# Moving one key unit from the pool branch to the output projection, splitting six mixed rows one tile earlier, and pooling before the last split, in a hybrid decoder step

## The chip, the cores and the metric

The kernel runs on one core of one Trainium2 chip. The metric is the device time of one execution in microseconds (us), lower being better. Engines are called PE (TensorE), DVE (VectorE), ACT (ScalarE), POOL (GpSimd) and SP (the queue that issues most DMAs); ACT has a DMA queue of its own, in order with its other work.

## What is computed

One inference step of one hybrid decoder layer, in float32, for 512 prompt tokens and 8 requests of 4 new tokens: 544 tokens of width 2048.

```python
h = rmsnorm(x, norm_mix)
proj = h @ w_in                                   # q | k | v | z_A | alpha | beta | u | z_B
...                                               # group A: gated delta rule on q, k, v -> o_a (1024 wide)
pooled, pool_new = multiscale_pool(proj[..., COL_U:COL_ZB], pool_buf, pos0, pool_w, pool_scale)
o_b = pooled * jax.nn.silu(proj[..., COL_ZB:])    # group B: trailing means over 2/4/8/16 tokens, a map per group
x = x + jnp.concatenate([o_a, o_b], axis=-1) @ w_out
h2 = rmsnorm(x, norm_cross)
qx = (h2 @ w_cq).reshape(bsz, t_len, X_HEADS, X_HEAD_DIM)
scores = jnp.einsum('bthd,bmhd->bhtm', qx, mem_k).astype(jnp.float32) * (X_HEAD_DIM ** -0.5)
probs = jax.nn.softmax(scores, axis=-1).astype(x.dtype)
ctx = jnp.einsum('bhtm,bmhd->bthd', probs, mem_v).reshape(bsz, t_len, D_MODEL)
x = x + ctx @ w_co
```

The new tokens attend to keys from a cache, `cache_mem_k`: 8 requests of 256 keys by 2048. They are stored key by key, and the score product needs them turned, width by key. Turning them is background work that the kernel spreads over earlier stages.

## The kernel before

**Tiles of three products.** Activations lie width by token, as 16 rows (row k is 128 widths by 544 tokens). A weight tile is 2048 by 128. A float32 product is made of three: each operand is split into a high part, rounded for PE, and a low part, the rest. ACT makes the high part of a weight tile (`cast_high`, L262), DVE the low part (`split_low`, L272), and PE multiplies high by high, high by low and low by high, for 16 rows and two halves of 272 tokens: 96 matmuls a tile (`multiply`, L288). Tiles are numbered through the kernel. Those of the pool branch are 64 to 79, four for each channel group g = 0 to 3 (two for z_B, q = 0 and 1, and two for u, q = 2 and 3); the output projection has 80 to 95; 96 to 99 begin the query projection, which then goes on with products of smaller parts (L2303). Results alternate between two pairs of PSUM banks, so the result of a tile must be read before PE begins the tile after next (`pj_read`).

**The order** is written out by hand: each engine has one list for each stage, and semaphores tie them. Each weight tile is loaded four tiles ahead by SP (`load_ahead`, L240). Beside the tiles of group g in the pool branch:

- In tiles q = 2 and 3 ACT copies u from PSUM to `ux` (L1762 to L1766), and only one `ux` exists: the second copy waits (`d_tile`) until DVE has made the pooled differences of the first (`dve_windows`, L1809 to L1822). POOL copies the new tokens from `ux` into `ucol` (L1873), and PE turns `ux` and `ucol` (`pe_ux`, L1879 and L1880) after row 4 of tile q = 3 for the first half of the group, and after row 11 of the next group's first tile for the second. For the last group that second turn stands after row 2 of tile 80.
- PE's map of the group (`pe_map`, L1892, 16 matmuls) comes in the next group's second tile; for the last group after row 7 of tile 80. DVE then finishes two of the rows `mixo` (L1831).
- The 16 rows `mixo` are the output projection's input. They are split in five parts: ACT's `mix_take_high` (L1794) and DVE's `mix_take_low` (L1799). Their order and their waits are a table, `MIX_PARTS`. Rows 0 to 5 of `mix_hi` lie where the key buffers `kin` and `kout` are, so that part waits for all stores of the pool branch's keys. Tile 80 starts when four parts are done, and its row 14 waits for the fifth.

```python
            pe.wait_ge(mix_low, 4)
                    steps = {2: [pe_ux(NG - 1, 1)], 7: [pe_map(NG - 1)], 13: [split(5)]}
```

**Keys.** A unit in the pool branch is 1024 widths of one request's 256 keys: 1 MB, four loads (L1646, two issued by SP and two by ACT), two turns on DVE (`dve_keys`, L1656), eight stores (L1652, half by SP and half by ACT). Step n = 4(g − 1) + q stores unit n − 1 and loads unit n, at the end of tile q's list on ACT, SP and DVE. A unit of the output projection (`load_late_units`, `dve_keys_late`) is half as large, 512 widths; step i stands at tile 80 + i, with its load in step i and its turn and stores in step i + 1. On DVE the turn stands ahead of the addition of that tile's result to the residual (`x`, L2021), on ACT the DMAs stand behind the normalised high part and the square of the result (L1997, L2000), and ahead of the cast of the weights of the tile after next. The query projection's DVE list (L2209 and on) follows directly on the last tile's.

Of the kernel before, what the change touches and what calls it, by code (L numbers as in the profile page):

```python
# [128 lines left out]
def build(nc, t):  # L129
    with ExitStack() as ctx:  # L130
# [9 lines left out]
        def area(start, end):  # L140

            pos = [start]

            def take(name, shape, dtype=F32):
                n = int(np.prod(shape))
                o = put(name, shape, dtype, pos[0])
                pos[0] += -(-n // 8) * 8
                assert pos[0] <= end, (name, pos[0], end)
                return o
            take.pos = pos  # L150
            return take
# [43 lines left out]
        def at_least(eng, s, v):  # L195

            if not (isinstance(v, int) and v <= 0):
                if isinstance(s, Reused):
                    eng.wait_ge(s.sem, s.at(v))
                else:  # L200
                    eng.wait_ge(s, v)
# [62 lines left out]
        def split_low(dve, stage, j, q):  # L264

            n = FIRST[stage] + j + q // 4
            q = q % 4
            if isinstance(n, int) and 4 * n >= NTILE:
                return
            dve.wait_ge(hi_cast, 4 * n + q + 1)  # L270
            lo, w = (low_wide, raw_wide) if is_mem(n) else (low, raw)
            dve.tensor_tensor(lo[q][:], w[q][:], high_of(n, q)[:].bitcast(F32), ALU.subtract).then_inc(lo_split, 1)  # L272
# [504 lines left out]
        def sample3(x):  # L777

            return x[:, SEQ:TOK].rearrange("p (b t) -> p b t", b=NB)
# [847 lines left out]
            "d_tile", "pw_loaded", "pooled", "ob_done", "mix_high", "mix_low", "old_rows"))  # L1627

        BLOCKS = MEM // T32
        POOL_UNITS = 10  # L1630
        OUT_UNITS = 12
        take = area(M_DELTA + 2 * 2 * P, M_HIMIX + 6 * TOK)
        kin = take("kin", [BLOCKS, 2 * P])
        kout = [take(f"kout{i}", [4, BLOCKS, T32]) for i in range(2)]
# [1 line left out]
        k_turned = Reused(conv_step, 9 * HEADS)  # L1636
        k_late_loaded = Reused(const_loaded, 16 + 64 * POOL_UNITS)
        k_late_stored = [Reused(xts_stored, 80 + 64 * POOL_UNITS), Reused(kts_stored, 64 + 64 * POOL_UNITS)]
        k_late_turned = Reused(conv_step, 9 * HEADS + 2 * POOL_UNITS)

# [7 lines left out]
        def keys_out(eng, src, b, tile, step, first, n, stored, quarters):  # L1648

            for i in quarters:  # L1650
                dst = keysT_d[b, first * T32:(first + n) * T32, tile + step * i, :].rearrange("(j d) m -> d j m", d=T32)
                eng.dma_start(dst, src[i * T32:(i + 1) * T32].rearrange("p j g m -> p j (g m)")).then_inc(stored.sem, 16)  # L1652
# [7 lines left out]
        def load_units(sp, n, quarters):  # L1660

            if 0 < n <= POOL_UNITS:
                sp.wait_ge(k_turned.sem, k_turned.at(2 * n))
                for f in range(2):
                    keys_out(sp, kout[f], (n - 1) // 2, 8 * ((n - 1) % 2) + f, 2, 0, 4, k_stored[f], quarters)
            if n < POOL_UNITS:
                if n == 0:
# [3 lines left out]
        def dve_keys(dve, n):  # L1671

            if 0 < n <= POOL_UNITS:
                dve.wait_ge(k_in_loaded.sem, k_in_loaded.at(64 * n))
                for f in range(2):
                    at_least(dve, k_stored[f], 64 * (n - 1))
                    keys_turn(dve, kout[f], kin[:, :, f * P:(f + 1) * P]).then_inc(k_turned.sem, 1)

        def u_sample(x):
            return x[:, BUF + SEQ:UN].rearrange("p (b s) -> p b s", b=NB)  # L1680
# [44 lines left out]
        def act_pool(act):  # L1725
            def body(g):
                first = is_first(g)
                for q in range(4):
# [15 lines left out]
                    if g == 1 and q == 2:  # L1744
                        mix_take_high(act, 0)
                    if g == 2 and q == 2:
                        mix_take_high(act, 1)
                    if g == 3 and q == 2:
                        mix_take_high(act, 2)
# [26 lines left out]
            act.activation(ust[0:BUF, 0, :], pj[0:BUF, 2 * i, 0:P], ACT.Copy)  # L1776
            act.activation(ust[0:NS, 1, :], pj[0:NS, 2 * i, P:2 * P], ACT.Copy).then_inc(ust_ready, 1)

        MIX_PARTS = ((6, 8), (8, 12), (12, 14), (0, 6), (14, 16))

        def mix_take_high(act, m):

            a, b = MIX_PARTS[m]
            if m in (0, 3):
                act.wait_ge(oa_done, HEADS)
            else:
                act.wait_ge(ob_done, (0, 4, 6, 0, 8)[m])
            if m == 3:
                for s in k_stored:
                    act.wait_ge(s.sem, s.at(64 * POOL_UNITS))  # L1790
                act.wait_ge(k_turned.sem, k_turned.at(2 * POOL_UNITS))
            if m == 4:
                act.wait_ge(ust_stored, 16 * 9 * 8)
            act.activation(mix_hi[:, a:b, :], mixo[:, a:b, :], ACT.Copy).then_inc(mix_high, 1)  # L1794

        def mix_take_low(dve, m):
            a, b = MIX_PARTS[m]
            dve.wait_ge(mix_high, m + 1)
            dve.tensor_tensor(mix_lo[:, a:b, :], mixo[:, a:b, :], mix_hi[:, a:b, :].bitcast(F32), ALU.subtract).then_inc(mix_low, 1)  # L1799

        def dve_windows(dve, g, i):

            n = 2 * g + i
            dve.wait_ge(pj_read, 4 * (16 + g) + 2 + i + 1)
            src = ux[:]
            for m in range(g + 1):
                dst = (us_a, us_b)[m % 2][:]
                lo = (2 << m) - 1
                dve.tensor_tensor(dst[:, lo:UN], src[:, lo:UN], src[:, lo - (1 << m):UN - (1 << m)], ALU.add).then_inc(win_step, 1)  # L1809
                wn[0] += 1  # L1810
                dve.wait_ge(win_step, wn[0])
                src = dst
            other = (us_b, us_a)[g % 2][:]
            if i == 0:
                at_least(dve, pooled, g)
            iw = 1.0 / WINDOWS[g]
            dve.tensor_tensor(other[:, 0:16], src[:, BUF:BUF + 16], cst[:, C_INV + 16 * g:C_INV + 16 * g + 16], ALU.mult).then_inc(win_step, 1)
            wn[0] += 1
            dve.wait_ge(win_step, wn[0])
            dve.tensor_tensor(dpool[:, i, 0:16], other[:, 0:16], ux[:, BUF:BUF + 16], ALU.subtract)  # L1820
            dve.scalar_tensor_tensor(dpool[:, i, 16:SEQ], src[:, BUF + 16:BUF + SEQ], iw, ux[:, BUF + 16:BUF + SEQ], ALU.mult, ALU.subtract)
            dve.scalar_tensor_tensor(sample3(dpool[:, i]), u_sample(src)[:, :, BUF:USEG], iw, u_sample(ux[:])[:, :, BUF:USEG],  # L1822
                                     ALU.mult, ALU.subtract).then_inc(d_tile, 1)
        wn = [0]

        def dve_map(dve, g):

            dve.wait_ge(pooled, g + 1)
            for d in range(2):
                o = halves(mixo[:, 8 + 2 * g + d, :])  # L1830
                dve.scalar_tensor_tensor(o, dk[:, 2 * d:2 * d + 2, 0:HALF], gain[:, G_POOL + 2 * g + d:G_POOL + 2 * g + d + 1],  # L1831
                                         o, ALU.mult, ALU.mult).then_inc(ob_done, 1)

        def dve_pool(dve):
            for g in range(NG):
                for q in range(4):
                    if g > 0:
                        split_low(dve, "pool", g, q + 1)
                    else:
                        dve_delta(dve, HEADS - 1, q, lambda: split_low(dve, "pool", 0, q + 1), lambda: None)  # L1840
                    if g > 0 and q == 0:
                        dve_windows(dve, g - 1, 1)
                    if g > 0 and q == 1:
                        dve_map(dve, g - 1)
                    if g > 0 and q == 2:
                        mix_take_low(dve, g - 1)
                    if q == 3:
                        if g == 3:
                            mix_take_low(dve, 3)
                        dve_windows(dve, g, 0)  # L1850
                    if g > 0:
                        dve_keys(dve, 4 * (g - 1) + q)

# [84 lines left out]
        def load_late_units(sp, i, quarters):  # L1938

            if 1 < i <= OUT_UNITS + 1:  # L1940
                sp.wait_ge(k_late_turned.sem, k_late_turned.at(2 * (i - 1)))
                b, h = divmod(2 * POOL_UNITS + i - 2, XH)
                for f in range(2):
                    keys_out(sp, kout_late[f], b, 4 * h, 1, 2 * f, 2, k_late_stored[f], quarters)
            if 0 < i <= OUT_UNITS:
                if i == 1:
# [4 lines left out]
        def dve_keys_late(dve, i):  # L1951

            if 1 < i <= OUT_UNITS + 1:
                dve.wait_ge(k_late_loaded.sem, k_late_loaded.at(64 * (i - 1)))
# [209 lines left out]
        def t_cast(act, S, idx):  # L2164
            kh, m = divmod(T_ORDER[idx], KH)
            act.wait_ge(S.t_step.sem, S.t_step.at(4 * idx + 4))
            if S is CQ and idx == 0:
                for s in k_late_stored:
                    act.wait_ge(s.sem, s.at(64 * OUT_UNITS))
            act.activation(q_t[kh][:, :, 0, m, :], q_tt[idx % 2][:], ACT.Copy).then_inc(S.t_high.sem, 1)  # L2170
# [136 lines left out]
        def sp_cq(sp):  # L2307
# [13 lines left out]
            for s in k_late_stored:  # L2321
                sp.wait_ge(s.sem, s.at(64 * OUT_UNITS))
            sp.wait_ge(part_done.sem, part_done.at(77))
# [864 lines left out]
```

## Time and profile before

| | |
|---|---|
| median of 3 runs | 1657.14 us (1656.83 to 1658.19) |
| the profiled execution | 1655.45 us |
| its span (first to last instruction) | 1653.6 us |
| granted TensorE clock, mean | 0.994 of full speed |
| PE busy | 1619.4 us, 98% of the span |
| pool branch, tiles 64 to 79 | about 765 to 971 us |
| output projection, tiles 80 to 95 | 975.7 to 1177.6 us |

The profile gives the busy time of each engine, who waited for whom, and each instruction with its start and length. A weight-tile matmul with 272 tokens starts 0.125 us after the one before it at full clock, though each is listed as longer, since they overlap. An idle PE is the one thing that counts directly; idle time elsewhere costs only if PE waits behind it.

### The profile page before, as it was taken

What the parts mean: (1) busy time and instruction counts of PE and PEld (TensorE: products, weight loads), DVE (VectorE), ACT (ScalarE), POOL (GpSimd) and SP (SyncE); (2) the same over time, 40 slices, a digit from 0 to 9 for tenths busy, and PEclk for the clock granted to TensorE, in tenths of its full rate; (3) what the DMA queues carried; (4) which work ended last, traced back from release to release, by engine and by line L of the source; (5) the groups of instructions that cost most, each with busy time, mean ns of one, the idle gap of its engine ahead of it and who ended that gap; (6) DMA issues with size and microseconds to landing.
All of it is one profiled execution on the core that took longest, in us unless ns stands there. A gap on an engine that the chain in (4) does not pass through costs nothing.

```text
span 1653.6 us, 31288 instructions
## 1 busy us (share of the span) xinstructions
PE 1619.4 (98%) x12650; PEld 1499.8 (91%) x12650; DVE 987.4 (60%) x1689; ACT 657.5 (40%) x1115; POOL 180.6 (11%) x191
## 2 busy tenths in 40 slices
PE   7999999999999999999999989999999999899998
PEld 5887899999999999999999989999999995499998
DVE  5676446765756647566344553444688853399952
ACT  5566345353452544425422222222343322235542
POOL 0121001111121111211100001111000000001120
PEclk9999999999999999999999999999999999999999
DMA  7898634233242432324389965787323359953462
GB/s 267 258 303 254 212 92 113 70 94 101 68 117 52 117 92 77 92 55 126 83 205 240 231 167 156 205 237 212 116 77 102 97 225 419 360 153 104 130 184 108
DMA packets 320670, 263.35 MB, mean 159 GB/s; under 512 B 15049, under 2 KB 287314, under 8 KB 315234
## 3 DMA queue, kind: packets, MB, share of 16 engines
q1 hardware_dynamic: 298752, 245.21, 49.9%
q10 hardware_dynamic: 21826, 16.87, 3.7%
q8 instruction: 63, 1.03, 0.3%
q14 instruction: 29, 0.24, 0.0%
HBM read 218.09 MB, written 44.30 MB: 159 GB/s over the span
## 4 chain that ended last, share of the span: by engine, by line
PE 84%; DVE 5%; DMA 4%; SPq 3%; ACT 1%; issue 1%; ACTq 1%; POOL 0%; DVEq 0%
PE pj L288 43%; PE pj L487 10%; PE pj L2303 7%; PE dk L2303 5%; DMA kin<-in_cache_mem_k_dram 2%; PE pj L3057 2%; PE dk L2567 2%; PE pj L2600 1%; DMA values_raw_b<-in_cache_mem_v_dram 1%; DVE kout L1656 1%; PE dk L1273 1%; PE pj L2578 1%; PE dk L1279 1%; SPq L1701 1%; PE dk L826 1%
## 5 line engine op out<-in xcount | busy, mean ns | idle before, releaser
L288 PE MATMUL pj<-a_hi,w_high 128*128 128x272 f32 x1792 | 394.1, 301 | 1.4 <-DVE w_low L272 1.4
L288 PE MATMUL pj<-a_hi,w_low 128*128 128x272 f32 x1792 | 370.2, 288 | 0.0
L288 PE MATMUL pj<-a_lo,w_high 128*128 128x272 f32 x1792 | 369.7, 288 | 0.0
L272 DVE TENSOR_TENSOR w_low<-w_raw,w_high 128x2048 fp32r<-128x2048 f32 x76 | 173.9, 2288 | 203.5 <-ACT w_high L262 203.4
L288 PEld LDWEIGHTS pj<-a_hi,w_high 128*128 128x128 f32 x1792 | 280.9, 189 | 15.0 <-issue 8.1
L288 PEld LDWEIGHTS pj<-a_lo,w_high 128*128 128x128 f32 x1792 | 281.6, 188 | 0.0
L288 PEld LDWEIGHTS pj<-a_hi,w_low 128*128 128x128 f32 x1792 | 280.2, 189 | 0.1
L262 ACT ACTIVATE w_high<-w_raw 128x2048 fp32r<-128x2048 f32 x76 | 145.5, 1915 | 140.9 <-issue 82.6
L288 PE MATMUL pj<-mix_hi,w_high 128*128 128x272 f32 x512 | 107.1, 291 | 4.0 <-issue 4.0
L2187 ACT ACTIVATE q_high<-q_part 128x512 fp32r<-128x512 f32 x140 | 77.5, 621 | 74.0 <-DVE q_part L2241 36.6
L288 PE MATMUL pj<-mix_lo,w_high 128*128 128x272 f32 x512 | 106.8, 290 | 0.0
L288 PE MATMUL pj<-mix_hi,w_low 128*128 128x272 f32 x512 | 106.2, 289 | 0.0
L272 DVE TENSOR_TENSOR w_low_wide<-w_raw_wide,w_high_wide 128x2048 fp32r<-128x2048 f32 x32 | 73.1, 2287 | 40.4 <-ACT w_high_wide L262 40.4
L2248 DVE TENSOR_TENSOR q_low<-q_part,q_high 128x512 fp32r<-128x512 f32 x140 | 93.0, 709 | 4.0 <-ACT q_high L2187 3.3
L288 PEld LDWEIGHTS pj<-mix_hi,w_high 128*128 128x128 f32 x512 | 81.5, 191 | 4.3 <-issue 4.2
L262 ACT ACTIVATE w_high_wide<-w_raw_wide 128x2048 fp32r<-128x2048 f32 x32 | 61.2, 1914 | 52.6 <-PE pj L487 44.0
L288 PEld LDWEIGHTS pj<-mix_hi,w_low 128*128 128x128 f32 x512 | 81.3, 190 | 0.0
L288 PEld LDWEIGHTS pj<-mix_lo,w_high 128*128 128x128 f32 x512 | 81.3, 191 | 0.0
L487 PE MATMUL pj<-w_high_wide,hm_lo 128*128 128x512 f32 x248 | 78.9, 399 | 0.0
L487 PE MATMUL pj<-w_high_wide,hm_hi 128*128 128x512 f32 x248 | 77.0, 391 | 0.0
L2241 DVE TENSOR_TENSOR q_part<-q_part 128x512 f32<-128x512 f32 x80 | 58.7, 734 | 22.1 <-DMA q_part<-in_w_cq_dram 17.8
L487 PE MATMUL pj<-w_low_wide,hm_hi 128*128 128x512 f32 x248 | 64.2, 394 | 0.0
(468 smaller groups left out, 2916.0 us busy)
## 6 DMA issues: line engine op xcount, KB each, us to landing
w_raw<-in_w_in_dram SPq DMA_DIRECT2D x48, 1024.0 KB, 6.0
w_raw_wide<-in_w_ck_dram SPq DMA_DIRECT2D x16, 1024.0 KB, 9.0
w_raw_wide<-in_w_cv_dram SPq DMA_DIRECT2D x16, 1024.0 KB, 7.1
w_raw<-in_w_out_dram SPq DMA_DIRECT2D x16, 1024.0 KB, 8.4
q_part<-in_w_cq_dram SPq DMA_DIRECT2D x48, 256.0 KB, 3.7
w_raw<-in_w_co_dram SPq DMA_DIRECT2D x8, 1024.0 KB, 6.2
q_part<-in_w_co_dram SPq DMA_DIRECT2D x32, 256.0 KB, 3.7
kin<-in_cache_mem_k_dram ACTq DMA_DIRECT2D x20, 256.0 KB, 6.2
```

The costliest lines, as they stand in the source:

```text
L262: act.activation(high_of(n, q)[:], w[q][:], ACT.Copy).then_inc(hi_cast, 1)
L272: dve.tensor_tensor(lo[q][:], w[q][:], high_of(n, q)[:].bitcast(F32), ALU.subtract).then_inc(lo_split, 1)
L288: mm = pe.matmul(pj[:, 2 * (q % 2) + b, 0:n], wt[:, k, :], x(k, o, n), start=(k == 0 and m == 0), stop=(k == KT - 1 and m == 2))
L487: mm = pe.matmul(pj[:, 2 * (j % 2) + m, :], x[:, KW * q + k, m * P:(m + 1) * P], wt[:, k, :], start=(q == 0 and u == 0), stop=(q == 3 and ...
L826: mm = pe.matmul(dk[0:64, b, 0:HALF], wt[:, k, :], x[:, k, b * HALF:(b + 1) * HALF], start=(k == 0 and m == 0), stop=(k == KT - 1 and m == 2))
L1273: mm = pe.matmul(dk[:, i, 0:HALF], ones, SQ[:, i // 2, (i % 2) * HALF:(i % 2 + 1) * HALF], start=True, stop=True)
L2187: act.activation(part_high[:, q_slot(n)], q_parts[G % 2][:, o], ACT.Copy).then_inc(S.part_cast.sem, 1)
L2241: dve.tensor_tensor(w[:, o], w[:, a], w[:, b], op).then_inc(S.part_step.sem, 1)
L2248: dve.tensor_tensor(part_low[G % 2][:, o], q_parts[G % 2][:, o], part_high[:, q_slot(n)].bitcast(F32), ALU.subtract).then_inc(S.part_split ...
L2303: mm = pe.matmul(q_bank(o), w[:, m, :], v, start=(kh == 0 and m == 0 and u == 0), stop=(kh == 1 and m == KH - 1 and u == 2))
L2567: mm = pe.matmul(scp(h)[:, i // 2, (i % 2) * 256:(i % 2) * 256 + 256], qx[:, DT * h + d, i * P:(i + 1) * P], ktb[h % 2][:, d, :], start=(d ...
L3057: mm = pe.matmul(half_product(u), wt[:, k, :], x[:, k, part], start=(k == 0 and m == 0), stop=(k == KT - 1 and m == 2))
```

## The change

Three edits, all in the lists around tiles 76 to 95.

1. `POOL_UNITS` goes from 10 to 9 and `OUT_UNITS` from 12 to 14: the last 1 MB unit of the pool branch becomes two of the output projection's half-size units. The keys turned are the same.
2. `MIX_PARTS` changes order: rows 0 to 5 are split third, in the third tile of the last group (tile 78), and rows 12 and 13 fourth, in tile 79. The waits in `mix_take_high` follow: the wait for the key stores now stands in tile 78's list.
3. In tile 79's list on DVE the pooling sums (`dve_windows(dve, 3, 0)`) come ahead of the fourth split.

```diff
-        POOL_UNITS = 10
-        OUT_UNITS = 12
+        POOL_UNITS = 9
+        OUT_UNITS = 14
...
-        MIX_PARTS = ((6, 8), (8, 12), (12, 14), (0, 6), (14, 16))
+        MIX_PARTS = ((6, 8), (8, 12), (0, 6), (12, 14), (14, 16))
...
-            if m in (0, 3):
+            if m in (0, 2):
                 act.wait_ge(oa_done, HEADS)
             else:
-                act.wait_ge(ob_done, (0, 4, 6, 0, 8)[m])
-            if m == 3:
+                act.wait_ge(ob_done, (0, 4, 0, 6, 8)[m])
+            if m == 2:
                 for s in k_stored:
                     act.wait_ge(s.sem, s.at(64 * POOL_UNITS))
...
                     if q == 3:
+                        dve_windows(dve, g, 0)
                         if g == 3:
                             mix_take_low(dve, 3)
-                        dve_windows(dve, g, 0)
```

**Where the instructions move.** PE's and POOL's lists are the same as before. First, ACT's list beside tiles 78 and 79, before and then with the change (`w_high_58<-w_raw_52` is tile 79's cast, `w_high_57<-w_raw_49` tile 80's; `128x3264` are six mixed rows, `128x1088` two):

```order
L262 ACTIVATE w_high_58<-w_raw_52 128x2048
L1794 ACTIVATE mix_hi<-mixo 128x1088
L1762 ACTIVATE ux<-pj 128x272
L1763 ACTIVATE ux<-pj 128x240
L1764 ACTIVATE ux<-pj 128x8x4
L1766 ACTIVATE ux<-pj 128x8x15
L1652 DMA keysT_scratch<-kout_161 32x4x256 x2
L1652 DMA keysT_scratch<-kout_162 32x4x256 x2
L262 ACTIVATE w_high_57<-w_raw_49 128x2048
L1776 ACTIVATE ust<-pj 15x128
L1777 ACTIVATE ust<-pj 32x128
L1794 ACTIVATE mix_hi<-mixo 128x3264
```

```order
L262 ACTIVATE w_high_58<-w_raw_52 128x2048
L1794 ACTIVATE mix_hi<-mixo 128x3264
L1762 ACTIVATE ux<-pj 128x272
L1763 ACTIVATE ux<-pj 128x240
L1764 ACTIVATE ux<-pj 128x8x4
L1766 ACTIVATE ux<-pj 128x8x15
L262 ACTIVATE w_high_57<-w_raw_49 128x2048
L1776 ACTIVATE ust<-pj 15x128
L1777 ACTIVATE ust<-pj 32x128
L1794 ACTIVATE mix_hi<-mixo 128x1088
```

The six rows stand now ahead of the first copy of u (tile 78), the two rows where the six were, and the DMAs of the removed unit are gone.

Second, the same place on DVE, as a difference (`w_low_53` is tile 80's low part), and where the two rows' split has gone:

```order
 L1656 STREAM_TRANSPOSE kout_162<-kin 128x8x4x32
 L272 TENSOR_TENSOR w_low_56<-w_raw_52,w_high_58 128x2048
-L1799 TENSOR_TENSOR mix_lo<-mixo,mix_hi 128x1088
-L1656 STREAM_TRANSPOSE kout_161<-kin 128x8x4x32
-L1656 STREAM_TRANSPOSE kout_162<-kin 128x8x4x32
-L272 TENSOR_TENSOR w_low_53<-w_raw_49,w_high_57 128x2048
 L1799 TENSOR_TENSOR mix_lo<-mixo,mix_hi 128x3264
+L272 TENSOR_TENSOR w_low_53<-w_raw_49,w_high_57 128x2048
 L1809 TENSOR_TENSOR us_a<-ux 128x678
 L1809 TENSOR_TENSOR us_b<-us_a 128x676
```

```order
 L1821 SCALAR_TENSOR_TENSOR dpool<-us_b,ux 128x496
 L1822 SCALAR_TENSOR_TENSOR dpool<-us_b,ux 128x32
+L1799 TENSOR_TENSOR mix_lo<-mixo,mix_hi 128x1088
 L1809 TENSOR_TENSOR us_a<-ux 128x678
 L1809 TENSOR_TENSOR us_b<-us_a 128x676
```

The six rows' split comes ahead of tile 80's weights, two turns are gone, and the two rows' split stands between the two pooling sums of the last group.

Third, DVE's last two tiles of the output projection (`w_low_56` and `w_low_53` are the weights of tiles 95 and 96; `x` and `a_lo` the results):

```order
 L2023 SCALAR_TENSOR_TENSOR a_lo<-x_1_166,gain,a_hi 128x544
 L272 TENSOR_TENSOR w_low_56<-w_raw_52,w_high_58 128x2048
+L1656 STREAM_TRANSPOSE kout_late_170<-kin_late 128x8x2x32
+L1656 STREAM_TRANSPOSE kout_late_171<-kin_late 128x8x2x32
 L2021 TENSOR_TENSOR x_0_165<-pj,xr_163 128x544
 L2023 SCALAR_TENSOR_TENSOR a_lo<-x_0_165,gain,a_hi 128x544
 L272 TENSOR_TENSOR w_low_53<-w_raw_49,w_high_57 128x2048
+L1656 STREAM_TRANSPOSE kout_late_170<-kin_late 128x8x2x32
+L1656 STREAM_TRANSPOSE kout_late_171<-kin_late 128x8x2x32
 L2021 TENSOR_TENSOR x_1_166<-pj,xr_164 128x544
 L2023 SCALAR_TENSOR_TENSOR a_lo<-x_1_166,gain,a_hi 128x544
```

Turns now stand ahead of the additions of tiles 94 and 95 as well; on SP and on ACT their loads and stores are added in tiles 93 to 95.

## Rows read from the trace of the kernel before

**Rows 1.** The page: busy time, share of the span and instructions of each engine.

```profile
PE 1619.4 (98%) x12650; PEld 1499.8 (91%) x12650; DVE 987.4 (60%) x1689; ACT 657.5 (40%) x1115; POOL 180.6 (11%) x191
```

**Rows 2.** Who PE waited for from 965 to 993 us: total, times, longest.

```profile
PE pj L288 <- issue: 4.0, 1, 4.0
PE pj L1879 <- POOL ucol L1873: 2.8, 1, 2.8
```

**Rows 3.** Timeline, PE: start us, us, line, operation [idle before <-releaser].

```profile
963.01 0.27 PE L1879 MATMUL pj<-cst,ux 128*15 128x128 f32 x1
...
970.99 0.41 PE L288 MATMUL pj<-a_lo,w_high 128*128 128x272 f32 x2
971.24 0.41 PE L288 MATMUL pj<-a_hi,w_low 128*128 128x272 f32 x2
975.67 0.49 PE L288 MATMUL pj<-mix_hi,w_high 128*128 128x272 f32 x2 [4.02 <-issue]
...
982.24 0.28 PE L1879 MATMUL pj<-cst,ux 128*15 128x128 f32 x1 [2.78 <-POOL ucol L1873]
...
987.76 3.83 PE L1892 MATMUL dk<-dpool,pw 128*128 128x272 f32 x16
```

**Rows 4.** Timeline, DVE, tiles 78 to 80.

```profile
960.72 2.37 DVE L1656 STREAM_TRANSPOSE kout<-kin 128x1024 f32<-128x1024 f32 x2 [0.58 <-DMA kin<-in_cache_mem_k_dram]
...
972.01 3.56 DVE L1799 TENSOR_TENSOR mix_lo<-mixo,mix_hi 128x3264 fp32r<-128x3264 f32 x1 [2.51 <-ACT mix_hi L1794]
975.49 0.86 DVE L1809 TENSOR_TENSOR us_a<-ux 128x678 f32<-128x678 f32 x1
...
979.95 0.18 DVE L1822 SCALAR_TENSOR_TENSOR dpool<-us_b,ux 128x32 f32<-128x32 f32 x1
981.25 0.87 DVE L1809 TENSOR_TENSOR us_a<-ux 128x678 f32<-128x678 f32 x1 [1.12 <-ACT ux L1766]
```

**Rows 5.** Timeline, ACT and its DMA queue (ACTq), tiles 77 to 80.

```profile
950.42 2.13 ACTq L1652 DMA_DIRECT2D keysT_scratch<-kout  x4
...
954.69 1.91 ACT L262 ACTIVATE w_high<-w_raw 128x2048 fp32r<-128x2048 f32 x1 [6.87 <-issue]
...
959.34 0.40 ACT L1762 ACTIVATE ux<-pj 128x272 f32<-128x272 f32 x1 [1.73 <-PE pj L288]
...
969.05 2.93 ACT L1794 ACTIVATE mix_hi<-mixo 128x3264 fp32r<-128x3264 f32 x1 [1.56 <-DMA keysT_scratch<-kout]
980.31 0.40 ACT L1762 ACTIVATE ux<-pj 128x272 f32<-128x272 f32 x1 [8.32 <-DVE dpool L1822]
```

**Rows 6.** Windows of PE: stretch, length, busy (instructions), granted clock, DMA share, GB/s.

```profile
976.30:979.50 3.20, 3.16 (x15) 0.52 0.14 35
...
987.00:1195.00 208.00, 208.00 (x1654) 1.00 0.66 185
```

**Rows 7.** The chain of waits, at the last key store: start us, us, what.

```profile
964.51 4.38 DMA keysT_scratch<-kout
```

**Rows 8.** The page, costliest groups: the low part of a weight tile.

```profile
L272 DVE TENSOR_TENSOR w_low<-w_raw,w_high 128x2048 fp32r<-128x2048 f32 x76 | 173.9, 2288 | 203.5 <-ACT w_high L262 203.4
```

**Rows 9.** Timeline, DVE, last tiles of the output projection, and the query projection.

```profile
1153.31 1.30 DVE L1656 STREAM_TRANSPOSE kout_late<-kin_late 128x512 f32<-128x512 f32 x2 [2.70 <-DMA kin_late<-in_cache_mem_k_dram]
...
1177.63 0.72 DVE L2021 TENSOR_TENSOR x<-pj,xr 128x544 f32<-128x544 f32 x1 [5.81 <-PE pj L288]
...
1223.20 2.50 DVE L2248 TENSOR_TENSOR q_low<-q_part,q_high 128x512 fp32r<-128x512 f32 x4
```

**Rows 10.** The chain of waits, where the query projection's small products begin.

```profile
1226.82 6.07 PE pj L2303 x48
```

**Rows 11.** Key stores of the pool branch: time from issue to landing.

```profile
DMA to landing us min/median/max: 2.0/3.1/6.0
```

**Rows 12.** Timeline, POOL, the last two copies of the new tokens.

```profile
960.32 0.21 POOL L1873 COPY ucol<-ux 128x32 f32<-128x32 f32 x1 [38.55 <-ACT ux L1766]
981.28 0.91 POOL L1873 COPY ucol<-ux 128x32 f32<-128x32 f32 x1 [20.75 <-ACT ux L1766]
```

**Rows 13.** Key loads of the output projection, the same.

```profile
DMA to landing us min/median/max: 2.3/4.0/8.1
```

## The prediction, made before the changed kernel ran

> **What bounds the kernel now.** I read the page first: PE is busy 1619.4 us, 98% of the span [rows 1], so only what shortens PE's list or removes its waits can count, and the change leaves PE's list as it is. The next view was who PE waited for. Around the change it waits twice [rows 2]: 4.0 us, put down to nothing, and 2.8 us for POOL's `ucol`. The timeline of PE shows where [rows 3]. Pairs of matmuls start 0.25 us apart at full clock, tile 79's last at 971.24, so tile 80 could start at 971.49; it starts at 975.67, 4.18 us late. What released it is on DVE: the low part of the six rows ends at 972.01 + 3.56 = 975.57 [rows 4], the fourth of the four parts that tile 80 waits for. Then 18 matmuls on (rows 0 to 2), PE's turn of `ux` waits 2.78 us, until 982.24, because the second copy of u starts only at 980.31 [rows 5], as soon as DVE has the pooled differences of the first, whose sums stood behind the six rows (975.49 to 980.13) [rows 4].
>
> These two waits cost more than their 7 us. After the first the granted clock is 0.52 of full speed, the 1.2 GHz level, with a half-idle PE behind it [rows 6]: 18 matmuls take 982.24 − 2.78 − 975.67 = 3.79 us, where at full clock they take 18 × 0.125 = 2.25. After the second, 30 matmuls up to the map (about 982.4 to 987.76) take 5.4 us instead of 3.75 [rows 3].
>
> Then I followed back why the six rows are late. ACT's high part of them starts at 969.05 [rows 5], 0.16 us after the last store of the last pool unit lands (964.51 + 4.38 = 968.89) [rows 7]. That unit is turned on DVE until 960.72 + 2.37 = 963.09 [rows 4]. So the chain is: turn, stores, high part, low part, then the sums, the copy, the turn of `ux`, the map.
>
> **The change, part by part.** Times are on the old profile's clock.
>
> *One pool unit fewer.* The last store is now unit 8's. Its turn ended at 950.4 already, for its stores are issued from 950.42 [rows 5]. From the end of the turn to the last landing it took 968.89 − 963.09 = 5.80 us for unit 9; the same from 950.4 gives 956.2. Unit 9's loads, which would have stood right behind these stores, and its turn of 2.37 us on DVE [rows 4] are gone.
>
> *Six rows in tile 78.* ACT casts tile 79's weights until at most 954.69 + 1.91 = 956.6, some 2 us earlier without the loads to issue ahead of it [rows 5], then waits for the landing and makes the high part from 956.35 to 959.3 (2.93 us). Queued behind it is the first copy of u, which starts at 959.34 today because tile 78 ends then [rows 5]: not later, but with no room. DVE makes the low part from 959.3 to 962.9 (3.56), where today two rows and the turn stand.
>
> *Tile 80's weights and the sums.* The low part of the weights takes 2.29 us [rows 8]: 962.9 to 965.2. The sums take 4.64 us (975.49 to 980.13) [rows 4]: to 969.8. Then the low part of two rows, a third of 3.56 or about 1.2 to 1.3 us: to 971.1. PE arrives at 971.49. The wait of 4.18 us is gone, with 0.4 us to spare. This is also what the third edit does: with the two rows first, the sums would end at 971.1, which still serves the copy.
>
> *Second copy of u.* It needs tile 79 finished (971.5) and the differences (969.8). From the copy's start to PE's turn it took 982.24 − 980.31 = 1.93 us, so the turn can go at 973.4; PE arrives at 971.49 + 2.25 = 973.74. The 2.78 us go, with 0.3 to spare. The second sums start 0.94 us after the copy (981.25 against 980.31) [rows 4, 5] and end 4.64 later, at 977.1; PE reaches the map at 973.74 + 0.22 for the two turns + 3.75 = 977.7, in time. Without waits I expect no fall of the clock.
>
> The sum: 4.18 + 2.78 + (3.79 − 2.25) + (5.4 − 3.75) = 10.1 us. Against it, the map starts at 987.76 now [rows 3] and at 977.7 then: 10.1. Behind the map the order is as it was, each on the other: no further gain.
>
> *Two late units more.* Turns of 1.30 us [rows 9] now stand ahead of the additions of tiles 94 and 95, and ACT and SP have stores and loads beside them. The same work stands beside each of the tiles 82 to 93 today, and PE was busy 208.0 of 208.0 us there [rows 6]; that is the cover. What is new is its end: DVE goes straight from tile 95 (addition at 1177.63) into the query projection and has no idle until the first low part there, done at 1223.20 + 2.50/4 = 1223.8 [rows 9]. PE needs it at 1226.82 [rows 10]. A delay of 1.3 us leaves 1.7. I cost it at nothing; if loads land so late that the slack is used up, each further us costs one.
>
> What stays unmeasured is the landing of unit 8's stores in its new role. Stores of this branch land 2.0 to 6.0 us after issue [rows 11]; I take the case of unit 9 (4.38 from issue), the nearest, with the same 1 MB weight load behind it. At 2.0 nothing more is won, as PE has no wait left: gain 10.1. At 6.0 everything in tile 78 is 1.6 us later.
>
> **The copy for the new tokens, and a rule that speaks against the change.** POOL's copy takes 0.21 us at 960.32, and 0.91 at 981.28, where it started 0.03 us after a DVE addition with two inputs in SBUF (981.25, 0.87 long) and ended 0.07 after it [rows 4, 12]. So I let a copy wait for such a DVE instruction. The six rows' subtraction is one, 3.56 us long, and it starts at 959.3, before the copy at 960.3. Then the copy ends not at 960.5 but at 962.9, and PE turns it at 963.01 [rows 3]: 0.1 us to spare instead of 2.5.
> The Trainium skill, "SBUF — State Buffer", section "Who interferes with whom", says that a DVE instruction with two SBUF inputs contends with a GpSimd instruction that reads SBUF, and that the later one fully blocks. By that rule the next rival is live; without it the sum would be 10.1 us in nearly all cases. The trace agrees (0.91 against 0.21).
>
> **The rivals.**
>
> A. *The forecast*: all waits at tile 80 go. 10.1 us. For it: four margins, each positive; against it: they are only 0.1 to 0.6 us.
>
> B. *A wait in tile 79 takes their place.* The store lands late, up to 957.8; high part until 960.9, low part until 964.5, the copy for the new tokens behind it, and PE, due at 963.01, waits up to 1.5 us in tile 79. The rest of the chain moves by as much and so does PE, so tile 80 still starts without a wait. If the clock falls too, 1.5 us more, as after the old waits. Gain 7.1 to 9.5; about 1649 us. For it: DMAs are dense there, and the margin is 0.1.
>
> C. *No change that can be told.* The 4.0 us wait has no releaser named [rows 2]; if something besides the six rows holds tile 80, or if a later stage that waits for loads gives the time back, under 3.3 us remain. Against it: 975.57 and 975.67 fit closely, and later loads are issued on signals of PE's progress, so they move with it. Time 1654 to 1657 us.
>
> D. *Slower, through the last late units.* DVE, in tile 95's list, sits on a key load that is late, with the addition, the next weights and the whole preparation of the query projection behind it. It decides from 1.7 us of lateness on; to be slower than before by 0.2% it must eat the 10.1 us as well: 1.7 + 10.1 + 3.3 = 15 us. Loads there land within 8.1 us of issue [rows 13] and are issued a tile (12 us) ahead: at worst they are about a microsecond late. Time 1660 us or more.
>
> **How the numbers follow.** The profiled execution took 1655.45 us, 1.7 under the median of 1657.14; its span is 1653.6. A: span 1643.5, so a profiled time of 1645.4 and a median of 1647.0. Chances: A 0.66, B 0.22, C 0.08, D 0.04. Within 0.2% (3.3 us) is about what a measurement of this kernel can tell from no change. A and B are faster by more (0.88), C is the same, D slower. The range takes A with the spread of the runs, down to 1645.6, and B to its bad end, 1657.14 − 7.1 = 1650.0, with a little spread: 1650.5. C and D stay outside.
>
> **What would show it.** In the new profile: no wait of PE at tile 80's start and at its turn of `ux`; full clock from 960 to 985; the six rows' high part starting near 956.3 and ending at about 959.3; the copy for the new tokens in tile 79 lasting some 2.5 us rather than 0.21 (that is B's door); the first key turn of the added units ahead of the additions of tiles 94 and 95, and no PE wait around the first small products of the query projection, some 10 us earlier than today. I am wrong if tile 80 still waits, if PE waits over 2 us in tile 79, or if the 10 us are there at tile 81 and no longer at the end.

## The result and the profile after

The changed kernel takes 1647.23 us, median of 5 runs (1644.57 to 1648.36), against 1656.83 us for the kernel before, run beside it, median of 5 (1654.52 to 1658.19). The ratio is 0.9942 with a 95% interval of 0.9931 to 0.9953: about 9.6 us faster. The span of the profiled execution is 1645.4 us, against 1653.6.

The first view is again who PE waited for, now from 900 to 1000 us in the changed kernel:

```profile
PE pj L288 <- DVE w_low L272: 0.8, 1, 0.8
```

Both waits of [rows 2] are gone. The one that is left stands before tile 77, where the kernel before waits as well; the change does not touch it. The timeline of PE, where [rows 3] were read (start, length, line, operation):

```profile
963.56 0.28 PE L1879 MATMUL pj<-cst,ux 128*15 128x128 f32 x1
...
971.80 0.42 PE L288 MATMUL pj<-a_hi,w_low 128*128 128x272 f32 x2
972.05 0.41 PE L288 MATMUL pj<-mix_hi,w_high 128*128 128x272 f32 x2
...
974.30 0.27 PE L1879 MATMUL pj<-cst,ux 128*15 128x128 f32 x1
...
978.27 2.00 PE L1892 MATMUL dk<-dpool,pw 128*128 128x272 f32 x8
```

Tile 80's first matmul (`mix_hi`) starts 0.25 us after tile 79's last pair, where it was 4.43 us. The turn of `ux` in tile 80 follows without a wait, and the map starts at 978.27, not 987.76. The windows of PE (stretch, length, busy, granted clock, DMA share, GB/s) show the clock of the stretch that [rows 6] had at 0.52:

```profile
976.30:979.50 3.20, 3.20 (x23) 1.00 0.39 98
960.00:985.00 25.00, 25.00 (x188) 1.00 0.37 101
987.00:1195.00 208.00, 207.22 (x1656) 1.00 0.68 194
```

Full clock and no idle from 960 to 985; but in the output projection PE was busy 207.22 of 208 us, where it had been 208.00. This wait is the larger part of what the gain lost again, and the experiments look at it.

ACT's timeline in the same place, for [rows 5]:

```profile
950.85 2.09 ACTq L1652 DMA_DIRECT2D keysT_scratch<-kout  x4
...
956.91 2.93 ACT L1794 ACTIVATE mix_hi<-mixo 128x3264 fp32r<-128x3264 f32 x1 [1.96 <-DMA keysT_scratch<-kout]
959.75 0.38 ACT L1762 ACTIVATE ux<-pj 128x272 f32<-128x272 f32 x1
...
964.32 1.10 ACT L1794 ACTIVATE mix_hi<-mixo 128x1088 fp32r<-128x1088 f32 x1
972.25 0.40 ACT L1762 ACTIVATE ux<-pj 128x272 f32<-128x272 f32 x1 [6.84 <-PE pj L288]
```

The six rows' high part starts at 956.91, released by the last key store, and the first copy of u stands right behind it. DVE and POOL, for [rows 4] and [rows 12]:

```profile
948.44 2.37 DVE L1656 STREAM_TRANSPOSE kout<-kin 128x1024 f32<-128x1024 f32 x2 [1.29 <-DMA kin<-in_cache_mem_k_dram]
...
959.87 3.56 DVE L1799 TENSOR_TENSOR mix_lo<-mixo,mix_hi 128x3264 fp32r<-128x3264 f32 x1 [2.60 <-ACT mix_hi L1794]
963.35 2.30 DVE L272 TENSOR_TENSOR w_low<-w_raw,w_high 128x2048 fp32r<-128x2048 f32 x1
965.57 0.85 DVE L1809 TENSOR_TENSOR us_a<-ux 128x678 f32<-128x678 f32 x1
...
970.12 1.28 DVE L1799 TENSOR_TENSOR mix_lo<-mixo,mix_hi 128x1088 fp32r<-128x1088 f32 x1
973.20 0.86 DVE L1809 TENSOR_TENSOR us_a<-ux 128x678 f32<-128x678 f32 x1 [1.80 <-ACT ux L1766]
```
```profile
960.70 2.80 POOL L1873 COPY ucol<-ux 128x32 f32<-128x32 f32 x1 [38.50 <-ACT ux L1766]
973.23 0.91 POOL L1873 COPY ucol<-ux 128x32 f32<-128x32 f32 x1 [9.73 <-ACT ux L1766]
```

The six rows' low part runs from 959.87 to 963.43, and POOL's copy for the new tokens, 0.21 us long before, now takes 2.80: it ends at 963.50, 0.07 us after the subtraction. PE turns it at 963.56. The turn comes 4.04 us after tile 79's start (959.52) where it came 3.87 us after (963.01 less 959.14): the margin of 0.1 us is used up, and no more than 0.17 us paid.

Four times tell where the time went. All are from profiles: the start of PE's small transpose ahead of tile 79, the addition of tile 80's result on DVE, the first small product of the query projection on PE, and the span.

| | tile 79 starts | addition of tile 80 | first small product | span |
|---|---|---|---|---|
| before | 959.14 | 997.63 | 1226.66 | 1653.6 |
| after | 959.52 | 988.14 | 1218.48 | 1645.4 |
| gained so far | −0.38 | 9.49 | 8.18 | 8.2 |

From tile 79 to the addition of tile 80 it took 38.49 us and takes 28.62: 9.87 less. From there to the first small product it took 229.03 and takes 230.34: 1.31 more. (Each is one execution. In the two later profiles of the changed kernel the first stretch takes 28.44 and 28.43 us, since the copy held nobody up there, and the second 229.02 and 229.03.)

### The profile page after: what moved, and what is told of

It is laid out like the page before. It is cut to its first block, busy times and chain, and to the rows that moved or that the text cites. A ratio compares the mean times of both kernels' runs of the same rounds, so it can differ in the third digit from the quotient of the medians.

```text
span 1645.4 us, 31303 instructions
## 1 busy us (share of the span) xinstructions
PE 1617.3 (98%) x12650; PEld 1497.8 (91%) x12650; DVE 988.1 (60%) x1691; ACT 657.5 (40%) x1115; POOL 183.4 (11%) x191
## 4 chain that ended last, share of the span: by engine, by line
PE 81%; DMA 7%; DVE 5%; SPq 2%; ACT 2%; issue 2%; ACTq 1%; POOL 0%; DVEq 0%
PE pj L288 39%; PE pj L487 10%; PE pj L2303 7%; PE dk L2303 5%; PE pj L3057 2%; DMA kin<-in_cache_mem_k_dram 2%; DMA xr<-xT_scratch 2%; PE dk L2567 2%; DMA kin_late<-in_cache_mem_k_dram 1%; PE pj L2600 1%; DMA values_raw_b<-in_cache_mem_v_dram 1%; PE dk L1273 1%; PE pj L2578 1%; ACTq L1652 1%; PE dk L1279 1%
```

## The experiments

### The first edit alone

Against the kernel before:

```diff
-        POOL_UNITS = 10
-        OUT_UNITS = 12
+        POOL_UNITS = 9
+        OUT_UNITS = 14
```

> Only the first edit: 9 pool units and 14 late units, the old order of the mixed parts and the sums last. My theory: with unit 9 gone the six rows in tile 79's list no longer wait for a store; ACT can start their high part right after the turned rows of tile 79 (about 964), the low part ends near 970.4, so tile 80 starts on time (the 4.2 us go), but the sums behind it end near 975, the second copy of u starts there, and PE waits some 3 us at its turn after row 2 of tile 80, with a fall of the clock of up to 1.5 us behind it. Gain over the kernel before 4 to 6 us: ratio about 0.997. Rival (the units are not what held the six rows, the order is): tile 80 still starts about 4 us late, ratio 1.000. Rival (the units alone bring everything): ratio 0.994.

Measured: median 1650.73 us, ratio 0.9968 (0.9956 to 0.9979), a gain of 6.5 us. The ten times are spread widely (1647.61 to 1655.38), and the profile is of the lowest of them, so the parts below are read from the stretch itself. The waits of PE from 820 to 1260 us, and DVE's timeline, show which of the two waits the unit had caused:

```profile
PE pj L1879 <- POOL ucol L1873: 3.0, 1, 3.0
PE pj L288 <- DVE w_low L272: 1.3, 1, 1.3
```
```profile
966.86 3.56 DVE L1799 TENSOR_TENSOR mix_lo<-mixo,mix_hi 128x3264 fp32r<-128x3264 f32 x1 [2.33 <-ACT mix_hi L1794]
970.33 0.86 DVE L1809 TENSOR_TENSOR us_a<-ux 128x678 f32<-128x678 f32 x1
...
974.79 0.19 DVE L1822 SCALAR_TENSOR_TENSOR dpool<-us_b,ux 128x32 f32<-128x32 f32 x1
```

The six rows' low part ends at 970.42 instead of 975.57, tile 80 starts on time, and the second wait stays, 3.0 us, since the sums behind that part end at 974.98. From tile 79's start to tile 80's addition it takes 990.94 − 959.29 = 31.65 us: 6.84 of the 9.87 us come from the first edit, the other 3.03 need the new order; the medians say the same (6.5 of 9.6). Both rivals fall. One detail was off: I had allowed up to 1.5 us for a fall of the clock behind the wait, and there was none:

```profile
974.00:977.00 3.00, 0.06 (x1) 1.00 1.03 286
977.10:984.00 6.90, 6.90 (x45) 1.00 0.19 47
```

### The third edit undone

Against the changed kernel:

```diff
                     if q == 3:
-                        dve_windows(dve, g, 0)
                         if g == 3:
                             mix_take_low(dve, 3)
+                        dve_windows(dve, g, 0)
```

> The changed kernel with its third edit undone: in tile 79 the two mixed rows' low part stands ahead of the pooling sums again. My theory: the sums then end about 1.3 us later, near 971.5, and the second copy of u waits for the end of tile 79 (971.9) anyway; tile 80 has its four parts sooner. No difference from the changed kernel: ratio to before 0.994. Rival (the third edit carries a part of the gain): PE waits 0.5 us or more at its turn in tile 80, and the ratio is 0.995 or above.

Measured: median 1648.59 us, ratio 0.9955 (0.9935 to 0.9975), which does not tell it from the changed kernel, though the ratio alone falls on the rival's side (0.995 or above). The profile speaks for the place itself: from tile 79 to tile 80's addition 987.52 − 959.08 = 28.44 us (28.62 in the changed kernel's first profile, 28.44 and 28.43 in its other two), and PE has no wait at its turn, which was the rival's other sign. The sums ended 970.50 + 0.18 = 970.7, while the copy that needs them started at 971.64, with the end of tile 79. So the third edit carries nothing here; it moves 1.3 us of DVE work within idle time. This profile lost its time later (232.19 us from tile 80's addition to the first small product, under lists that the third edit does not touch), in the output projection; its waits of PE from 820 to 1260 us:

```profile
PE pj L288 <- DVE w_low L272: 1.5, 4, 0.6
PE pj L2303 <- DVE q_low L2248: 1.1, 1, 1.1
```

The second row is PE at the first small product of the query projection, where my fourth rival stood.

### The turn of tile 79 two rows earlier, and its control

The same edit, once against the changed kernel and once against the kernel before:

```diff
-                steps[3].setdefault(4, []).append(pe_ux(g, 0))
+                steps[3].setdefault(4 if first else 2, []).append(pe_ux(g, 0))
```

> The changed kernel with PE's turn of ux in the tiles q = 3 of groups 1 to 3 moved from after row 4 to after row 2, 1.5 us earlier. My theory (POOL's copy is held until the six rows' subtraction on DVE has ended): in tile 79 the copy ends near 963.5, PE arrives at about 962.0 and waits 1.5 us; perhaps a fall of the clock behind it. Slower than the changed kernel by 1.5 to 3 us: ratio to before 0.995 to 0.996. In groups 1 and 2 there is no such subtraction beside it and no wait. Rival (the copy is only listed as long, its result is there 0.2 us after its start): no wait of PE, ratio 0.994.

> The control: the same earlier turn in the kernel before, where no DVE subtraction runs beside the copy in tile 79. The copy ends at about 960.5 and PE comes at 961.5: no wait in tile 79, the copy 0.21 us long, time as before (within 1 us).

Measured on the changed kernel: median 1647.2 us, ratio 0.9949 (0.9929 to 0.9969). POOL's copy, the subtraction on DVE and PE's turn in tile 79:

```profile
960.60 2.81 POOL L1873 COPY ucol<-ux 128x32 f32<-128x32 f32 x1 [38.72 <-ACT ux L1766]
```
```profile
959.78 3.56 DVE L1799 TENSOR_TENSOR mix_lo<-mixo,mix_hi 128x3264 fp32r<-128x3264 f32 x1 [2.29 <-ACT mix_hi L1794]
```
```profile
963.46 0.28 PE L1879 MATMUL pj<-cst,ux 128*15 128x128 f32 x1 [1.68 <-POOL ucol L1873]
```

and in the control, on the kernel before:

```profile
960.60 0.21 POOL L1873 COPY ucol<-ux 128x32 f32<-128x32 f32 x1 [38.56 <-ACT ux L1766]
```
```profile
961.85 0.27 PE L1879 MATMUL pj<-cst,ux 128*15 128x128 f32 x1
```

Both copies start at 960.60. With the subtraction beside it the copy takes 2.81 us and ends at 963.41, 0.07 after it, and PE waits 1.68 us for it; without, 0.21 us and no wait. The copy's result is really late, not only listed so. All nine profiles in which the subtraction began first show the same: the copy takes from 1.42 to 2.81 us, depending on when it starts, and ends 0.06 to 0.08 us after the subtraction. The stretch up to tile 80's addition is 989.56 − 959.26 = 30.30 us, 1.86 more than the 28.44 of the changed kernel's undisturbed profiles. PE's turn stands 1.83 us behind its place (961.38 + 0.25 to 963.46), so the wait is all of it, and the granted clock from 963.4 to 967.0 us is 1.00. The medians do not separate 1.7 us here, for the times vary by as much; the control's single run took 1658.75 us, 1.6 above the median of the kernel before beside it where I had expected 1 at most, with 231.54 us from tile 80's addition to the first small product (998.13 to 1229.67), though it has only the twelve late units.

### Do the added units cost anything?

> The changed kernel once more, as the measure for the three beside it. Its part up to tile 80 takes what it took (addition of tile 80 near 988). What I look at is the stretch from that addition to the first small product of the query projection: 230.5 us in the changed kernel's profile, 229.2 in the one before; I expect 229 to 232, changing from run to run with where loads land.

Without the two units, against the changed kernel:

```diff
-        OUT_UNITS = 14
+        OUT_UNITS = 12
...
-            sp.dma_start(kept_keys[slot][:, first:end, :], keysT_d[b, :, first:end, :]).then_inc(kv_loaded[slot].sem, 16)
+            sp.dma_start(kept_keys[slot][:, first:end, :], keysT_d[0 if b == NB - 1 else b, :, first:end, :]).then_inc(kv_loaded[slot].sem, 16)
```

> The changed kernel without its two added late units: 9 pool units and 12 late ones; the last 1024 widths of the last request's keys are not turned, and that request is scored with keys of the first in their place. My theory: the two added units cost about 1 us, by DVE entering the query projection later and by tiles 94 and 95; this kernel is 0.5 to 1.5 us faster than the changed one beside it, and has no wait at the first small product. Rival (the added units are free, the loss of 1.3 us is the loads of the other twelve): same as the changed kernel within 0.4 us, with PE waits for low parts still there in tiles 83 to 93.

Measured: the changed kernel again 1647.11 us, ratio 0.9936 (0.9922 to 0.9949); without the two units 1647.45 us, ratio 0.994 (0.9927 to 0.9954). My expectation of 0.5 to 1.5 us fell. Without the units, the stretch from tile 80's addition to the first small product is 1220.08 − 991.05 = 229.03 us; with them, in this second profile of the same kernel, 1217.30 − 988.28 = 229.02. So the added units need not cost anything. The first profile lost 1.31 us all the same: 0.90 ahead of tile 95 (first row), 0.19 ahead of tile 94, and 0.2 that I cannot place. DVE's rows, and below them one of ACT's DMA queue, show what led to it:

```profile
1157.15 0.52 PE L288 MATMUL pj<-mix_hi,w_high 128*128 128x272 f32 x2 [0.75 <-DVE w_low L272]
```
```profile
1135.24 0.72 DVE L2021 TENSOR_TENSOR x<-pj,xr 128x544 f32<-128x544 f32 x1 [1.43 <-issue]
...
1147.93 1.30 DVE L1656 STREAM_TRANSPOSE kout_late<-kin_late 128x512 f32<-128x512 f32 x2 [3.85 <-DMA kin_late<-in_cache_mem_k_dram]
1149.15 0.69 DVE L2021 TENSOR_TENSOR x<-pj,xr 128x544 f32<-128x544 f32 x1
...
1154.80 2.29 DVE L272 TENSOR_TENSOR w_low<-w_raw,w_high 128x2048 fp32r<-128x2048 f32 x1 [3.36 <-ACT w_high L262]
```
```profile
1151.69 1.06 ACTq L1646 DMA_DIRECT2D kin_late<-in_cache_mem_k_dram  x2
```

In the kernel before, the same low part, of tile 95's weights, waits a microsecond less for ACT's high part:

```profile
1159.09 2.29 DVE L272 TENSOR_TENSOR w_low<-w_raw,w_high 128x2048 fp32r<-128x2048 f32 x1 [2.27 <-ACT w_high L262]
```

In the changed kernel's profile, tile 92's addition had waited 1.43 us for something without a name (the residual's load, as the next experiment shows) and started 3.1 us after its tile's end, so ACT's high part, its stores and its key load came late. The key load landed for a turn at 1147.93, 3.8 us after tile 93's end (1144.14, as tiles end 12.00 us apart from 988.14 on); the addition behind the turn was 5.0 us late, and the low part of tile 95's weights ended at 1157.09, 0.9 us after PE could have begun. Up to here this is work that the old unit counts have too: the turn at 1147.93 is of the twelfth late unit. But beside tile 93 ACT now also issues the thirteenth unit's loads (1.06 us) ahead of the cast of tile 95's weights; without an added unit DVE waits 2.27 us for that cast in the kernel before and 2.53 us in the version with twelve, with it 3.36 us. Some 0.8 to 1.1 us earlier, the low part would have cost PE next to nothing. So the 0.9 us at tile 95 took both: a chain late by old work, and an added unit's loads on top. In each of these profiles the lateness is handed from tile to tile, through additions, DMAs and turns, and what PE sees of it differs.

### Residual loads earlier, turns behind the additions

First on SP alone, against the changed kernel:

```diff
-                    sp_residual(sp, "out", j, q)
+                    i = 4 * j + q
+                    if i == 0:
+                        sp_residual(sp, "out", 0, 0)
+                        sp_residual(sp, "out", 0, 1)
                     if q or not is_first(j):
                         sp.wait_ge(pj_read, 80 + 4 * j + q)
                         sp_x2(sp, j if q else j - 1, (q - 1) % 4)
+                        if i < 15:
+                            sp_residual(sp, "out", (i + 1) // 4, (i + 1) % 4)
```

Then the same, and on DVE besides:

```diff
-                    dve_keys_late(dve, i)
                     dve.wait_ge(tile_done, 80 + i + 1)
...
                     dve.tensor_tensor(halves(x2[q % 2][:]), product(q), halves(xr[q % 2][:]), ALU.add).then_inc(pj_read, 1)
+                    dve_keys_late(dve, i)
```

> The changed kernel with SP's load of the residual row for tile 80+i issued one tile earlier (right behind the store of the result two before it), so that it is no longer behind the 1 MB weight load. My theory: the addition then never waits for this load (9.8 us in six waits in the changed kernel), only for key turns; PE's waits for low parts in the output projection go in part. Gain 0 to 1.3 us on the changed kernel. Rival (the key loads alone set the pace): no difference, and additions as late as before.

> The same, and on DVE the key turns behind the addition of the tile instead of ahead of it, in the gap in which DVE waits for ACT's high part. My theory: additions start with the end of their tile in all 16 tiles, ACT's list follows, no PE wait for a low part between tile 81 and the first small product; stretch 229 us or less. Gain on the changed kernel 0.5 to 2 us. Rival (the stores and loads of the keys now come later, so that turns and the low parts behind them are late instead): no gain, PE waits for low parts as before.

Measured: 1646.41 us, ratio 0.9934 (0.9921 to 0.9948), and 1645.7 us, ratio 0.9928 (0.9914 to 0.9941). DVE's waits from 985 to 1185 us in the first of the two:

```profile
DVE kout_late L1656 <- DMA kin_late<-in_cache_mem_k_dram: 30.9, 14, 3.0
DVE x L2026 <- PE pj L288: 14.6, 9, 5.8
```

No addition (now L2026) waits without a name any more, where the changed kernel had six such waits of 9.8 us in all: what they had waited for was the residual's load. With both edits, the waits and the first and the last three additions (now L2025):

```profile
DVE x L2025 <- PE pj L288: 50.4, 16, 5.8
```
```profile
987.73 0.72 DVE L2025 TENSOR_TENSOR x<-pj,xr 128x544 f32<-128x544 f32 x1 [2.05 <-PE pj L288]
...
1143.72 0.73 DVE L2025 TENSOR_TENSOR x<-pj,xr 128x544 f32<-128x544 f32 x1 [2.84 <-PE pj L288]
...
1155.72 0.73 DVE L2025 TENSOR_TENSOR x<-pj,xr 128x544 f32<-128x544 f32 x1 [2.84 <-PE pj L288]
...
1167.72 0.73 DVE L2025 TENSOR_TENSOR x<-pj,xr 128x544 f32<-128x544 f32 x1 [2.83 <-PE pj L288]
```

All 16 additions start with the end of their tile, 12.00 us apart, and none waits for a key load. In both profiles the stretch is 229.03 us (987.96 to 1216.99, 987.73 to 1216.76), without a wait of PE in it. To see whether that is time won, the last pair ran again beside the changed kernel:

> The changed kernel a third time, beside the next one, to tell apart 1.4 us. Ratio to before 0.9935 to 0.9945; the stretch from tile 80's addition to the first small product is 229 to 232 us.

> The version with the residual loads one tile earlier and the key turns behind the additions, a second time. My theory: all 16 additions 12.00 us apart again and the stretch 229.0 us, so this kernel's times are lower by about 1 us in the middle and spread less than the changed kernel's beside it; ratio to before 0.992 to 0.994. Rival (the first comparison was luck): the two medians lie within 0.5 us, or the additions are uneven again.

Measured: the changed kernel 1645.78 us, ratio 0.9934 (0.9922 to 0.9946); the version with even additions 1645.74 us, ratio 0.9935 (0.9922 to 0.9948). The rival holds: the medians are 0.04 us apart, and the stretch was 229.03 us in both profiles (989.13 to 1218.16 and 988.21 to 1217.24). The even order does in each of its profiles what it should, but often there is nothing to remove. In six profiles with 14 units and the old order in this stage, the changed kernel's three among them, the stretch was 229.0 (three times), 230.1, 230.3 and 232.2 us; in three with twelve, 229.0, 229.0 and 231.5. Above 229.03 that is 0.9 us in the mean with 14 and 0.8 with twelve, so a price of the added units is not shown; nor is it ruled out, for two of the six waited at the first small product (1.1 and 0.3 us) and none of the three did. No version was shown to beat the changed kernel.

Not tried: the second edit without the first. With ten pool units ACT's wait for the last unit's stores would stand ahead of that unit's turn on DVE, which itself stands behind the split that ACT must feed; the lists would wait on each other.

## Why the prediction was right

The median was forecast at 1647.0 and is 1647.23; forecast A is what happened. That the median is met within 0.3 us is luck. The span was worked out as 1643.5 and is 1645.4, and the 1.9 us between have three parts: 0.38 because tile 79 started that much later in this profile, 0.23 because the gain around tile 80 was 9.87 and not 10.1, and 1.31 lost in the output projection. The first is scatter ahead of the change: tile 79 starts anywhere from 959.08 to 962.61 in the twelve profiles. The median comes out right because I added 1.7 us to the profiled time, as the first profile of the kernel before lay that much below its median; here the profiled execution is the median. The gain, from kernels run side by side, is 9.6 us of the 10.1 forecast.

- *What holds tile 80.* The wait had no name in [rows 2]; I took the six rows' low part for it, from 975.57 against 975.67. Shown: with the low part ending at 970.42 in the first experiment, the wait is gone.
- *The landing of unit 8's stores.* Taken as 5.80 us after the turn's end, as for unit 9. The turn ended at 948.44 + 2.37 = 950.81 and the high part started at 956.91, so 6.1 less the 0.16 between landing and start: about 5.9. This and 0.4 us of general lateness brought everything in tile 78 half a microsecond (0.56) behind my times. PE was only 0.38 behind, and the difference is what its turn in tile 79 waited.
- *POOL's copy held by the subtraction.* Right, with its size: forecast to end 0.07 after it, and it ends 0.06 to 0.08 after it in nine profiles, with a control. The rule of the Trainium skill's page "SBUF — State Buffer", section "Who interferes with whom", that a DVE instruction with two SBUF inputs contends with a GpSimd one that reads SBUF, holds in this kernel: 2.81 us against 0.21. Rival B was as near as its margin said: the turn came 0.17 us later than undisturbed, and with PE 1.5 us earlier it waited 1.68 us.
- *The second copy and the map.* Forecast 973.74 and 977.7, measured 974.30 and 978.27: both 0.56 late, as tile 79's turn was by 0.55. These margins held; only that of the first copy did not quite.
- *The clock.* Of the 10.1 us, 3.2 were for matmuls at the lower clock. The measured 9.87 contain them; idle alone was 6.8. I had also allowed 1.5 us of clock for the shorter wait of rival B, and as much for the wait left in the first experiment; this was wrong: waits of 1.68 and 3.03 us left it at full speed.
- *The third edit.* I said that either order serves the copy. Shown: 28.44 us without it, 28.43 to 28.62 with it.
- *The late units.* Costed at nothing, with the cover that the same work stands beside tiles 82 to 93 unharmed. This is the weakest term of the sum. In the best profiles it holds (229.02 and 229.03 with and without), and the mean over the profiles shows no price. But PE's 208.00 of 208.0 us in [rows 6] was one execution, and I took it for a property of the kernel: the control with the old unit counts lost 2.5 us there. I looked for the end of the added work only in DVE's list at the first small product, where I counted 1.7 us left; with the first small product at 1226.66, not at the 1226.82 of [rows 10], it was 1.5. That was used up in two of six profiles with 14 units (waits of 1.1 and 0.3 us), so rival D's mechanism exists; it needed 15 us and shows one. What I named and gave no price is ACT's list: the added loads ahead of the cast for tile 95 were a condition of the 0.9 us in the changed kernel's first profile. And a late load took up to 9.2 us from issue there, not the 8.1 that I took as the worst.

## What to carry to other kernels

When a hand-ordered list keeps an engine waiting, look for the piece of background work whose completion the wait really needs; moving one unit of it to a stage with room brought 6.8 us, and the new order of what stood behind it 3.0. Check, in each place that a long two-input DVE operation moves to, which small GpSimd copies run beside it and who waits for them. A stage with no wait in one profile is not a stage with slack: compare several profiles of the same kernel before a loss of a microsecond is put down to an edit, and look also in the lists of the engines that only issue the added DMAs.

## What the hardware showed that I had not expected

The first wait of PE cost more than its length, and a shorter one cost nothing more. In the kernel before, some 3 us more went to matmuls at the 1.2 GHz level. The granted clock was 0.52 from 976.3 to 979.5 us [rows 6], behind the wait of 4.0 us and ahead of the second; it was 0.61 from 982.4 to 986.4, behind the second wait, of 2.8 us, 18 matmuls on. The control, with waits of 4.2 and 2.5 us in the same places, shows 0.50 and 0.53. A single wait of 3.0 us at the same turn, with tile 80 begun in time, was followed by full clock, and so was one of 1.7 us. So the first fall needs no second wait beside it. The second fall came behind a wait shorter than one that cost nothing by itself, and what the first wait did to it is not shown.

The landing of like loads spreads widely within one execution: in the three profiles of the changed kernel the late key loads, of 128 KB each, took 2.4 to 2.6 us from issue at the least, 3.4 to 3.5 in the median, and 9.2, 8.6 and 8.2 us at the most. With residual loads earlier and turns behind the additions the slowest took 6.4 and 7.1 us.
